# Reordering VectorE, ScalarE and TensorE queues in the mixer's tail of a two-layer fp32 decoder trunk

## What is computed

```python
h = modulate(x, 1)
q, k, v, u, gates = jnp.split(h @ w_in[l], SPLITS, axis=-1)
# rotary on q and k; 12 heads in 3 groups of dilated causal windows; the groups merged by their softmax sums
y_attn = o @ attn_wo[l]
# conv_module: gated linear unit of u, 31-tap depthwise causal convolution, LayerNorm, SiLU, then a product:
y_conv = conv_module(u, conv_w[l], conv_b[l], conv_ln_g[l], conv_ln_b[l], conv_wo[l])
g_attn, g_conv = jnp.split(gates, N_BRANCH, axis=-1)
y = jax.nn.sigmoid(g_attn) * y_attn + jax.nn.sigmoid(g_conv) * y_conv
x = x + gate(1) * (y @ w_out[l])
```

## Time and profile before

| | before |
|---|---|
| median of 3 runs | 1280.22 us (1279.88 to 1281.08) |
| the profiled execution | 1281.08 us, its span 1279.3 us |
| PE busy | 1234.3 us, 96% |
| DVE busy | 965.5 us, 75% |
| ACT busy | 546.9 us, 43% |
| mean granted TensorE clock | 0.995 |

### The profile page before, as it was taken

How to read it: one execution, slowest core, us unless ns; L and a number is a source line. 1 busy time by engine, 2 the same in 40 slices (tenths; PEclk the granted TensorE clock), 3 DMA queues, 4 the chain that set the end, 5 groups by cost and what they waited for, 6 DMA issues and landing times.

```text
span 1279.3 us, 13844 instructions
## 1 busy us (share of the span) xinstructions
PE 1234.3 (96%) x5440; PEld 957.3 (75%) x5448; DVE 965.5 (75%) x1341; ACT 546.9 (43%) x576; POOL 2.2 (0%) x5
## 2 busy tenths in 40 slices
PE   3999999999999999999999999999999999999997
PEld 2588887766776887888878888876676678888885
DVE  5698886699997576988668888668999866644443
ACT  3343434532344555344355433354323564634431
POOL 0000000000000000000000000000000000000000
PEclk9999999999999999999999999999999999999999
DMA  9989994444233539889747889545532335455540
GB/s 375 416 317 373 375 377 177 184 179 166 100 113 118 191 111 377 345 342 356 301 170 276 343 344 356 193 162 204 188 133 99 132 132 196 167 197 189 193 177 34
DMA packets 52913, 293.44 MB, mean 229 GB/s; under 512 B 6640, under 2 KB 6896, under 8 KB 27120
## 3 DMA queue, kind: packets, MB, share of 16 engines
q1 hardware_dynamic: 51120, 289.38, 60.4%
q10 hardware_dynamic: 1728, 3.17, 0.7%
HBM read 291.45 MB, written 1.07 MB: 229 GB/s over the span
## 4 chain that ended last, share of the span: by engine, by line
PE 90%; DVE 3%; DMA 3%; ACT 2%; issue 1%; SPq 0%; DVEq 0%
PE ps L329 24%; PE ps L331 24%; PE ps L330 24%; PE ps L348 12%; DMA raw<-in_weights 2%; PE ps L515 1%; PE ps L396 1%; PE ps L537 1%; DMA ada_raw<-in_ada_w 1%; DVE hF L1084 1%; PE ps L526 0%; PE ps L485 0%; ACT L715 0%; DVE w_lo L997 0%; PE ps L380 0%
## 5 line engine op out<-in xcount | busy, mean ns | idle before, releaser
L997 DVE TENSOR_TENSOR w_lo<-raw,w_hi 128x2048 fp32r<-128x2048 f32 x176 | 401.0, 2286 | 40.8 <-ACT w_hi L709 40.5
L709 ACT CAST w_hi<-raw 128x2048 fp32r<-128x2048 f32 x176 | 334.5, 1910 | 163.7 <-PE ps L331 82.9
L329 PE MATMUL ps<-w_hi,hA_hi 128*128 128x512 f32 (+1 forms) x992 | 397.7, 401 | 2.9 <-DVE hA_lo L997 2.9
L331 PE MATMUL ps<-w_hi,hA_lo 128*128 128x512 f32 (+1 forms) x992 | 385.2, 388 | 0.0
L330 PE MATMUL ps<-w_lo,hA_hi 128*128 128x512 f32 (+1 forms) x992 | 384.6, 388 | 0.0
L329 PEld LDWEIGHTS ps<-w_hi,hA_hi 128*128 128x128 f32 x992 | 187.4, 189 | 46.6 <-issue 11.9
L330 PEld LDWEIGHTS ps<-w_lo,hA_hi 128*128 128x128 f32 x992 | 187.7, 189 | 38.5 <-issue 3.3
L331 PEld LDWEIGHTS ps<-w_hi,hA_lo 128*128 128x128 f32 x992 | 187.2, 189 | 38.9
L1186 DVE SCALAR_TENSOR_TENSOR work<-conv_in,par,work 128x256 f32<-128x256 f32 x480 | 193.7, 478 | 0.0
L1012 DVE SCALAR_TENSOR_TENSOR product<-ada_raw,c_bc 128x1024 f32<-128x1024 f32 x144 | 171.6, 1220 | 15.6 <-DMA ada_raw<-in_ada_w 15.2
L348 PE MATMUL ps<-raw,hF 128*128 128x512 f32 x384 | 171.6, 598 | 5.5 <-ACT hF L734 5.5
(11 more groups left out here) (120 smaller groups left out, 741.8 us busy)
## 6 DMA issues: line engine op xcount, KB each, us to landing
raw<-in_weights SPq DMA_DIRECT2D x200, 1024.0 KB, 4.8
ada_raw<-in_ada_w SPq DMA_DIRECT2D x144, 512.0 KB, 6.7
gate_bc<-gate_scratch ACTq DMA_DIRECT2D x6, 512.0 KB, 6.3
x<-in_x_tok SPq DMA_DIRECT2D x1, 1024.0 KB, 7.4
out_tok<-xn_h SPq DMA_DIRECT2D x4, 256.0 KB, 2.2
c_bc<-in_c_row SPq DMA_DIRECT2D x1, 512.0 KB, 4.4
c_bc<-in_g_row SPq DMA_DIRECT2D x1, 512.0 KB, 5.6
mask_all<-in_mask SPq DMA_DIRECT2D x1, 416.0 KB, 16.3
```

The source lines that it names most:

```text
L329: nc.tensor.matmul(out_ap, stat[0], mov[0], start=start, stop=False)
L331: return nc.tensor.matmul(out_ap, stat[1], mov[0], start=False, stop=stop)
L709: nc.scalar.copy(w_hi[:, s % HI, :], raw[:, p % RAW, :]).then_inc(hi_done, 1)
L997: return nc.vector.tensor_tensor(dst, whole, hi_part.bitcast(F32), ALU.subtract)
```

## The change

Six places of the mixer's lists are reordered; no instruction is added, removed or changed in shape. On PE, both token tiles of panel 25 come ahead of `ln_turn(1)`. On ACT, `hi(base + 26)` comes ahead of `turned(3)`, and the copy of the fourth gate group comes ahead of the third of the four SiLU pairs. On DVE, `lo(base + 27)` comes ahead of the LayerNorm's reciprocals, `lo(base + 28)` takes its old place, and `merged(1, 1)` comes ahead of `y_low(0)` and `y_low(1)`.

```diff
@@ TensorE
                 group(M_G3, 0, 2)
                 ln_turn(0)
-                group(M_G3 + 1, 1, 2, (0,))
+                group(M_G3 + 1, 1, 2)
                 ln_turn(1)
-                group(M_G3 + 1, 1, 2, (1,))
@@ ScalarE
                 exps(3)
                 gate_copy(1)
+                hi(base + 26)
                 turned(3)
-                hi(base + 26)
@@ ScalarE
                 for i in range(4):
+                    if i == 2:
+                        act_e.wait_ge(panel_done, base + M_G3 + 2)
+                        nc.scalar.copy(gates[:, :, 1536:2048], ps[:, 2:4, :]).then_inc(g3_done, 1)
                     act_e.wait_ge(bT_done, 4 * l + i + 1)
...
-                act_e.wait_ge(panel_done, base + M_G3 + 2)
-                nc.scalar.copy(gates[:, :, 1536:2048], ps[:, 2:4, :]).then_inc(g3_done, 1)
@@ VectorE
+                lo(base + 27)
                 for tt in range(TT):
                     dve.wait_ge(ln_std, 2 * l + tt + 1)
                     nc.vector.reciprocal(rstd[:, tt:tt + 1], std[:, tt:tt + 1]).then_inc(ln_rstd, 1)
...
-                lo(base + 27)
+                lo(base + 28)
                 for i in range(4):
...
-                    if i == 1:
-                        lo(base + 28)
@@ VectorE
                 merged(1, 0)
+                merged(1, 1)
                 y_low(0)
                 y_low(1)
-                merged(1, 1)
```

## The result

The changed kernel takes 1295.72 us (median of four runs, 1293.88 to 1296.83) against 1280.34 for the kernel before: 1.0121 times as long, 95% interval 1.0109 to 1.0134. The forecast was 1295.7. With fifteen further executions on record it takes 1293.50 to 1298.78, median of all nineteen 1295.81.

What follows compares the result with a forecast made beforehand. TensorE's waits and clock bound the kernel. New waits of 1.62 + 1.86 + 2 x 1.48 + 2 x 2.71 = 11.86 us plus 3.68 of clock drops make 15.5, from 1280.22 to 1295.7 us; range 1289 to 1302.

Steps and rivals of the forecast that it cites:

- What bounds the kernel: Whole kernel: TensorE is busy 96% of a 1279.3 us span, so only its waits or slowing count.
- Part 1: ACT's hi(base+26) ahead of turned(3): waits for panel 26's DMA, delaying PE's pv(3) by 1.62 and 1.86 us.
- Part 2: DVE's lo(base+27) ahead of the reciprocals, lo(base+28) in its place: hidden, with 0.6 us to spare.
- Part 3: Panel 25 ahead of ln_turn(1), gates copy ahead of SiLU 3: PE waits 1.48 us on hA_lo each layer.
- rival F: ACT's table switches take longer behind the new order, merged(0,1) comes late: 1297.1 us, or 1297.5 with drain; 2%.
- Part 4: DVE's merged(1,1) ahead of both y_low: PE's first w_out waits 2.71 us on hB_lo in each layer.
- The clock: Behind the hB_lo wait: one added clock drop of 1.84 us per layer; old drops at conv_turn(3) stay.
- rival B: Shorter stalls of 1.4 to 1.9 us also draw clock drops: 1299.4 us, or 1303.1 for all four; 15%.
- rival A: The last stall, at w_out, draws no clock drop, or an old drop goes: 1292.1 us; 19%.
- C: The pv(3) stall is taken back at conv_turn(3), idle shrinking to 0.8 us without a drop: 1288.5 us; 9%.
- D: Faster: idle and drop at conv_turn(3), 8.7 us, go; 1277.9 us with the w_out stall covered; 2%.
- E: The reordering does nothing because all moved steps are in PE's shadow: 1280.2 us; 3%.

Runs made afterwards that it cites:

- the run with a landed panel: Kernel before with ACT's hi(base+26) ahead of turned(3), but casting the long-landed panel 25 instead of 26: 1280.18 us, 0.9997 times before.
- the four steps early: Kernel before with DVE's last four convolution steps ahead of the first LayerNorm statistics and the product that waits for PE: 1273.95 us, 0.9947 times before.
- ACT's half of part 3: Kernel before with only the copy of the gates moved ahead of ACT's third SiLU pair: 1287.40 us, 1.0047 times before.
- PE's half of part 3: Kernel before with only both token tiles of panel 25 moved ahead of ln_turn(1): 1283.40 us, 1.0019 times before.

## Why the prediction was right, point by point

**What bounds the kernel.** Right: the loss came from PE's waits and clock. DVE's and ACT's new idle times of 4 to 5 us show in the time only through PE.

**Part 1**, forecast +1.62 and +1.86. Idle of 1.45 and 1.50 measured. The cause was right and is shown by the run with a landed panel. The term was 0.2 to 0.4 too large: I spaced ACT's instructions at 1.93 behind a 1.91 cast and 0.60 between the two copies, as they stood when each waited for something; queued behind one another they start 1.81 and 0.37 apart.

**Part 2**, forecast 0. Right to 0.3 us. The 0.6 us of slack were read behind a clock drop, which had made PE ask 1.6 us later; in the three cases without the drop the slack was gone and `ln_turn(0)` came 0.26 us late, in layer 0 of the changed kernel too.

**Part 3**, forecast +1.48. Measured 1.42 and 1.44, and the halves 1.0 and 2.3 against 0.9 and 2.35. The slack of 2.5 us that decides it was read correctly. ACT's table switch took 419.43 to 420.73, 1.30 us, so the 1.38 us of drain that the Trainium skill's page "ScalarE: Activation LUTs", section "What ACT_TABLE_LOAD costs", adds to each switch did not show behind the new order either. The measurement decides, and rival F fell.

**Part 4**, forecast +2.71 of wait, measured 2.71 in both layers and in every run that had it.

**The clock**, forecast one more drop in each layer, 3.7 us. This is the step that was right only in kind, off both in number and in price. The profiled execution has one more drop than before, not two, and not where I put both: one of two behind `hB_lo`, one behind `pv(3)`, which rival B held, and one of the old two missing, as in rival A. As for the price, from the end of the wait at `conv_turn(3)` PE's four transposes and 24 matmuls take 7.70 to 7.77 us in the 13 cases with a drop and 6.11 to 6.14 in the seven without: a drop costs 1.6 us. The prediction's 1.84 compared with a stream that had no wait before it, so it holds 0.2 us that come with every wait. The term was too large for this execution by one drop, 1.6 us.

**What the sum lacked.** PE restarts slowly: at full clock the first matmul behind a wait takes 0.50 or 0.47 us of the chain instead of 0.23, and `pv(3)` takes 2.22 instead of the 1.96 of the earlier trace rows. Part of it is lost overlap: in the stream a row lasts 0.39 us and 0.16 of it lie under its neighbour. The 24 matmuls behind a wait without a drop take 5.69 to 5.74 us, where 24 x 0.227 is 5.45. Six new waits times 0.26 are 1.6 us; the forecast held some 0.2 of it in each 1.84 and nothing for the other four waits. With it the profiled span closes: 11.2 us of new idle time (1.45 + 1.50 + 1.42 + 1.44 + 2.71 + 2.71), 1.6 of restarts, 1.6 of one net drop and 0.3 of part 2 are 14.7, less 0.6 by which PE's other waits shrank: 14.1 against 14.2.

So the hit on the median, 15.5 against 15.4, is partly luck. Against the profile the forecast is 1.3 us too high: idle times 0.6 too long, one drop too many and the shrunken other waits outweigh the missing restarts and part 2. It met the median because the timed runs lie 15.4 above the kernel before where this profile shows 14.2. How many drops the timed runs had cannot be read without a profile; their mean clock does not tell it, since 4 of the 13 profiles also have a clock of 0.50 in the start-up, between 21 and 30 us, and all have it in the last microseconds of the program.

**The rivals.** C is refuted: in every kernel with part 1 and the old order of the steps, `conv_turn(3)` still waits 2.5 us. D's place was the right one to look at: with the four steps early, idle and drops there go and 6.5 us come back, against the 7.7 that 2 x (2.0 + 1.84) would give. With the drop at 1.6 us and present in 13 of 20 cases, 2 x (2.0 + 0.65 x 1.6) estimates 6.1. But the change does not touch this place. Of A and B each came half true, as said under the clock, and E fell with every part but the second.

## What to carry to other kernels

An instruction may be brought forward only as far as its own last input allows: in front of that, it starts no sooner and everything queued behind it on its engine starts later. Before moving a step, read when its input lands (a DMA, a panel finished) and who waits for the ones it passes; parts 1 and 4 and ACT's half of part 3 lost in that one form, and the gain was its reverse, four ready steps taken out from behind a wait. PE's half of part 3 is another form: nothing was missing where the group was moved to, but it made `ln_turn(1)` 3.4 us later, and what hung on that had 2.5 us of slack. A slack that was read in a stretch at the low clock is not there when the drop does not come, as part 2 shows. On a TensorE that is otherwise never idle, price a wait at its length, plus the slow first matmul (0.26 us here), plus a clock drop with a chance, not a certainty.

## What the runs showed of the hardware

**The same wait draws a clock drop in some executions and not in others.** Counted over the profiles of all kernels of the study: behind the 2.5 us wait of `conv_turn(3)` the clock fell in 13 of 20 cases; behind the 2.7 us of `hB_lo` in 4 of 6; behind the 1.3 to 1.5 us of `pv(3)` in 3 of 8; behind the 1.4 to 1.5 us of `hA_lo` in none of 8, and behind its 2.3 us in none of 2 (of whose kernel the other timed runs were slower). Waits that the change does not touch, 1.35 us for `xn_h` and 1.57 us for `mid_lo`, drew none in 39 and 13 cases. The length of the wait alone does not order these: 2.3 us at one place drew none, 1.3 us at another did. Around `pv(3)` PE runs 64-column products and small transposes, around `hA_lo` 512-column matmuls; no run here tests whether that is the reason. A drop cost 1.6 us at `conv_turn(3)` (7.74 us against 6.12, medians of the 13 and the seven cases) and 1.5 to 1.6 us behind `hB_lo`.

**A restart costs about 0.26 us** of the first instructions behind a wait, at full clock, in addition to the wait itself: `pv(3)` 2.22 us against 1.96, 24 matmuls 5.69 to 5.74 against 5.45.

**Single profiles differ by more than a wait before they reach the change.** PE reaches the matmul behind the first `mid_lo` between 55.5 and 57.2 us in the 13 profiles, whose instructions are the same up to there. Two profiles are therefore compared stage by stage, and kernels by the medians of their runs.
